# Three attentions of a two-block network on one core: the masks are added on VectorE, in the operation that finds each row's maximum, and no longer by products on TensorE

## What is computed

```
FOX (16 heads of 64): s = q.k * scale + log_f_cum[query] - log_f_cum[key];  keys after the query masked (causal)
MLA (8 heads, query and key of 96, values of 64): s = q.k;   keys of later chunks of 64 masked
SPA (8 heads of 64):  s = q.k;   only the 128 keys with the highest index score of each query are kept
p = softmax(where(mask, s, -inf));   o = p @ v
```

## Time and profile before

| | |
|---|---|
| median of 3 runs | 1862.43 us (1858.46 to 1863.55) |
| profiled execution, its own time | 1852.84 us |
| its span, first to last instruction | 1851.0 us |
| TensorE busy | 1765.5 us, 95% |
| VectorE, ScalarE, GpSimd busy | 666.1, 643.6, 696.8 us |
| mean granted clock of TensorE | 0.987 |

### The profile page before, as it was taken

The page is one execution under the profiler, slowest core; times in us unless marked ns, Lnnn a source line. Parts: engine busy times, 40 slices in busy tenths (PEclk is TensorE's granted clock), DMA queues, the critical chain, the costliest instruction groups (busy, mean ns, idle before and its releaser), DMA issues. The chain is left out here.

```text
span 1851.0 us, 24083 instructions
## 1 busy us (share of the span) xinstructions
PE 1765.5 (95%) x9646; PEld 1488.6 (80%) x9646; DVE 666.1 (36%) x1087; ACT 643.6 (35%) x957; POOL 696.8 (38%) x522
## 2 busy tenths in 40 slices
PE   5999999899999999999999999999999989899999
PEld 5777899688888887878898888888887877668777
DVE  3449236320100013232454400100115179798441
ACT  4643534332222224324333522222225222346440
POOL 2523233254444554543200444444553455620002
PEclk9999999999999999999999999999999999999999
DMA  4112112122322232231200222233222222210001
GB/s 182 69 46 92 69 47 92 57 92 91 108 96 102 91 106 87 103 114 66 74 1 1 92 91 91 92 112 113 91 92 101 92 101 81 93 44 24 1 1 46
DMA packets 22467, 145.40 MB, mean 79 GB/s; under 512 B 2640, under 2 KB 3280, under 8 KB 6384
## 3 DMA queue, kind: packets, MB, share of 16 engines
q1 hardware_dynamic: 22384, 144.22, 21.8%
HBM read 142.05 MB, written 2.10 MB: 78 GB/s over the span
## 5 line engine op out<-in xcount | busy, mean ns | idle before, releaser
L2302 POOL TENSOR_TENSOR wlo<-wraw,whi 128x512 fp32r<-128x512 f32 (+2 forms) x500 | 678.5, 1389 | 1102.1 <-ACT whi L132 1102.1
L132 ACT ACTIVATE whi<-wraw 128x2048 fp32r<-128x2048 f32 (+2 forms) x125 | 235.3, 1883 | 330.5 <-PE PS L329 193.0
L425 PE MATMUL PS<-hT_hi,whi 128*128 128x512 f32 x704 | 274.0, 389 | 0.0
L426 PE MATMUL PS<-hT_lo,whi 128*128 128x512 f32 x704 | 273.9, 389 | 0.0
L427 PE MATMUL PS<-hT_hi,wlo 128*128 128x512 f32 x704 | 273.9, 389 | 0.0
L1511 DVE TENSOR_TENSOR act_sb<-sil,PS 128x512 f32 x44 | 30.3, 688 | 427.4 <-ACT sil L1487 427.4
L425 PEld LDWEIGHTS PS<-hT_hi,whi 128*128 128x128 f32 x704 | 132.2, 188 | 27.5
L427 PEld LDWEIGHTS PS<-hT_hi,wlo 128*128 128x128 f32 x704 | 132.2, 188 | 27.4
L426 PEld LDWEIGHTS PS<-hT_lo,whi 128*128 128x128 f32 x704 | 132.2, 188 | 27.1
L1487 ACT ACTIVATE sil<-PS 128x512 f32<-128x512 f32 x44 | 26.4, 599 | 355.4 <-PE PS L427 335.5
L458 PE MATMUL PS<-whi,hT_hi 128*128 128x512 f32 (+2 forms) x320 | 122.8, 384 | 12.2 <-POOL wlo L2302 4.3
(11 more groups left out here) (366 smaller groups left out, 3164.3 us busy)
## 6 DMA issues: line engine op xcount, KB each, us to landing
wraw<-wpack SPq DMA_DIRECT2D x125, 1024.0 KB, 4.8
gain<-gains SPq DMA_DIRECT2D x10, 512.0 KB, 6.1
x_sb<-x SPq DMA_DIRECT2D x8, 512.0 KB, 7.3
out<-x_sb SPq DMA_DIRECT2D x4, 512.0 KB, 2.6
csb<-consts SPq DMA_DIRECT2D x1, 768.0 KB, 6.7
vlat<-vecs SPq DMA_DIRECT2D x1, 320.0 KB, 3.4
vh<-vecs SPq DMA_DIRECT2D x1, 96.0 KB, 3.9
small<-vecs SPq DMA_DIRECT2D x1, 80.0 KB, 11.5
```

The source lines that it names most:

```text
L132: act.activation(whi[q % 2][:, w], wraw[q % 2][:, w], ACT.Copy).then_inc(w_hi, 1)
L425: nc.tensor.matmul(o, whi[q][w], hT_hi[:, k, :], start=(k == 0), stop=False)
L426: nc.tensor.matmul(o, whi[q][w], hT_lo[:, k, :], start=False, stop=False)
L2302: p.tensor_tensor(wlo[q][:, a:b], wraw[q][:, a:b], whi[q][:, a:b].bitcast(F32), ALU.subtract).then_inc(w_lo, 1)
```

## The change

The mask products are gone, and a unit's scores are one product over all its columns. VectorE's TENSOR_REDUCE becomes a tensor_tensor_reduce: it adds scores and mask, multiplies by -1 and writes the result back in place in PSUM, and writes the minimum over the row (which is the negated maximum) as a second output. exp then reads its input with a scale of -1. For the masks to cover all columns of a unit, FOX and the chunk mask get a tile of 512 columns each, zeros in 384 and the diagonal block in the last 128, of which a unit reads the last (i+1) x 128; VectorE makes them with a memset and a copy each. SPA's mask tiles become float32, the fp32r identities are gone, and the wait for SPA's masks moves from TensorE's to VectorE's queue.

```diff
@@ pe_scores
-                if self.ready and h % 8 == 0 and i:
-                    self.ready(i)
-                full, m = self.mask(i)
                 b, q = self.ring(u)[0], self.q(h, i)
-                n, d = (i + 1) * P, i * P
-                if full:
-                    t.matmul(PS[:, b, 0:n].rearrange("p (j c) -> p j c", c=P), q, self.k(h, 0, i + 1), start=True, stop=False)
-                    t.matmul(PS[:, b, 0:n], identr[:, :], m, start=False, stop=True).then_inc(sem("at_score"), 1)
-                else:
-                    if i:
-                        t.matmul(PS[:, b, 0:d].rearrange("p (j c) -> p j c", c=P), q, self.k(h, 0, i), start=True, stop=True)
-                    t.matmul(PS[:, b, d:n], q, self.k(h, i, i + 1), start=True, stop=False)
-                    t.matmul(PS[:, b, d:n], ident, m, start=False, stop=True).then_inc(sem("at_score"), 1)
+                t.matmul(PS[:, b, 0:(i + 1) * P].rearrange("p (j c) -> p j c", c=P), q, self.k(h, 0, i + 1), start=True,
+                         stop=True).then_inc(sem("at_score"), 1)
@@ exp
-                a.activation(self.pbuf[m][:, 0:n], PS[:, b, 0:n], ACT.Exp, bias=self.nm[:, u % 4:u % 4 + 1],
+                a.activation(self.pbuf[m][:, 0:n], PS[:, b, 0:n], ACT.Exp, bias=self.nm[:, u % 4:u % 4 + 1], scale=-1.0,
                              accum_out=self.rs[:, u:u + 1]).then_inc(sem("at_exp"), 1)
@@ dve_max
-                v.tensor_reduce(self.nm[:, u % 4:u % 4 + 1], PS[:, self.ring(u)[0], 0:(self.units[u][1] + 1) * P], AX_X,
-                                ALU.max, negate=True).then_inc(sem("at_max"), 1)
+                _, i, h = self.units[u]
+                if self.ready and h % 8 == 0 and i:
+                    self.ready(i)
+                s = PS[:, self.ring(u)[0], 0:(i + 1) * P]
+                v.tensor_tensor_reduce(out=s, in0=s, in1=self.mask(i), scale=-1.0, scalar=-MAX_NEG, op0=ALU.add, op1=ALU.min,
+                                       accum_out=self.nm[:, u % 4:u % 4 + 1]).then_inc(sem("at_max"), 1)
@@ setup of the attentions
-        identr = at("identr", AT_JUNK, [P, P], F32R)
+        masks = [at("causal", AT_ARENA + 86 * KB, [P, SEQ]), at("chunks", AT_JUNK + 2 * KB, [P, SEQ])]
+
+        def dve_mask(n, diagonal):
+
+            v = nc.vector
+            v.memset(masks[n][:, 0:SEQ - P], 0.0).then_inc(dve_step, 1)
+            v.tensor_copy(masks[n][:, SEQ - P:SEQ], const(diagonal)).then_inc(dve_step, 1)
+            stepped(2)
+
+        def mask_row(n, i):
+            return masks[n][:, (TT - 1 - i) * P:SEQ]
@@ dve_foxproj
             v.memset(QA[64:66, :, :], 1.0).then_inc(sem("rows1"), 1)
+            dve_mask(0, "negcausal")
             NQ.dve_xn(0)
@@ second block
-        topm = [at(f"topm{i}", AT_XN + 2 * KB * i, [P, SEQ], F32R) for i in range(3)]
+        topm = [at(f"topm{i}", AT_XN + 2 * KB * i, [P, SEQ]) for i in range(3)]
@@ dve_index
-            v.tensor_copy(identr[:, :], ident).then_inc(sem("mask"), 1)
+            dve_mask(1, "negchunk")
@@ mask_a, MLA, SPA (FOX and MLA: lambda i: mask_row(0, i) and mask_row(1, i))
-            return (True, topm[i - 1][:, 0:(i + 1) * P]) if i else (False, const("negchunk"))
+            return topm[i - 1][:, 0:(i + 1) * P] if i else mask_row(1, 0)
-                        ready=lambda i: nc.tensor.wait_ge(sem("mask"), 5 - i))
+                        ready=lambda i: nc.vector.wait_ge(sem("mask"), 4 - i))
```

More of the change, by code:

```diff
@@ L1691, in program @@
                         lambda h, a, b: KA[0:66, h, a * P:b * P].rearrange("p (j c) -> p j c", c=P), lambda h, j: FV[:, j, h * FD:(h + 1) * FD],
-                        lambda i: (False, const("negcausal")),
+                        lambda i: mask_row(0, i),
                         lambda i, b: QA[:, 4 * b:4 * b + 4, i * P:(i + 1) * P].rearrange("p a (b c) -> p a b c", b=2),
@@ L2173, in program @@
         MLA = Attention([FOX], BH, lambda h, i: qb[0:BQ, i, h, :], lambda h, a, b: kb[0:BQ, a:b, h, :],
-                        lambda h, j: vb[:, j, h, :], lambda i: (False, const("negchunk")), out_view, pbuf, ptbuf,
+                        lambda h, j: vb[:, j, h, :], lambda i: mask_row(1, i), out_view, pbuf, ptbuf,
                         after=after_out(1), copies="scalar")
```

## The result

The changed kernel takes **1885.70 us**, the median of 4 runs (1881.17 to 1889.51), beside 1860.45 for the kernel before on the same chip: a ratio of 1.0133, 95% interval 1.0104 to 1.0162. It is slower, by 25 us, where 1846 and a gain were forecast. The profiled execution took 1889.51 us, its span is 1887.7.

What follows compares the result with a forecast made beforehand. TensorE, busy 95% of the span, was taken as the bound, limited in MLA and SPA by the chain ending in ScalarE's copy. Gains 10.2 + 0.6 + 5.9 = 16.7 us off median 1862.43 gave 1846; range 1838 to 1857.

Steps and rivals of the forecast that it cites:

- the one sentence on the clock: Small units: more TensorE waiting might drop the clock to 1.2 GHz, costing a few us, within the range.
- the sum: Gains of FOX, MLA and SPA added: 10.2 + 0.6 + 5.9 = 16.7 us off the median 1862.43.
- TensorE's share in FOX, 0.22 a unit: FOX: dropping two mask passes over 128 columns saves 0.22 us a unit; units of i=3 go from 2.42 to 2.20.
- FOX's units of i=0: FOX's smallest units: no shorter than now; 13 x (0.04 - 0.12) = -1.0 us, 3 x 0.22 = 0.7.
- slack: Time from the end of the copy of turned weights to values(n-2)'s first weight load, less 0.05; zero where TensorE waits.
- x: VectorE's maximum: extra time of the new operation over TENSOR_REDUCE on the chain; 0.12 us, from 0 to 0.25.
- Rival 4: VectorE's new operation runs at half the column rate, adding 0.26 to 0.66 us a unit: 1870 us; chance 0.07.
- rival 3: VectorE's accumulator read-out is dear, 0.25 to 0.4 us: 1853.5 at 0.25, middle 1857; chance 0.15.
- the slower side: Whole kernel: a measured time slower than before, given 0.07; its mechanism was the half column rate on VectorE.
- 5.9 us in the sum: SPA's forecast gain: 2.2, 3.0, 1.0 and -0.3 us for i of 3, 2, 1 and 0.
- 0.6 us in the sum: MLA's forecast gain: 1.1 us for i=3, 0.7 for i=2, -0.6 each for i=1 and i=0.
- 10.2: FOX's forecast gain in us: 10.6 for units of i=3, 2 and 1, with -1.0 and 0.7 for i=0.

Runs made afterwards that it cites:

- MLA by products: Changed kernel with MLA put back to its mask products and plain reduce, FOX and SPA new: 1839.81 us, 0.9893.
- all rows: Changed kernel with score products of all three attentions over 128 rows, query rows beyond the head's own zero: 1829.22 us, 0.9832.
- pause ahead of FOX: Kernel with all score products over 128 rows, TensorE made to wait for six GpSimd fills at the start of FOX: 1843.79 us, 0.9927.
- MLA alone over 128 rows: Changed kernel with only MLA's score products over 128 rows instead of 96, SPA with its 64: 1876.37 us, 1.0093, one execution 1964.31.
- product and sum: Changed kernel with MLA's mask products back on TensorE and VectorE's new operation kept, mask added twice: 1850.94 us, 0.9952.
- FOX over 128 rows: Changed kernel with FOX's score products over 128 rows, MLA as before, SPA new over 64 rows: 1841.01 us, 0.9893.
- second series: Kernel with all score products over 128 rows run once more, 5 runs: 1834.33 us, 0.985 against the kernel before.

## Why the prediction was wrong

**The step that failed** is the one sentence on the clock: "TensorE will wait more in the small units than it does now; should the clock fall to the 1.2 GHz level there, that costs a few us and belongs to the range." It rightly saw that the clock could fall and priced the fall as if the clock came back with the next stretch of work, as it does in the short spells of the projections. The runs show that here the way back is missing: 119.5 us at half rate, from 1718.2 to 1837.7, SPA 94.4 us long for 59.6. The projections' spells are 3.4 and 6.8 us in the kernel before; this one ended when SPA did. I took the clock as a matter of how busy TensorE is, and looked at one stretch at 1.00; what rows the products use did not enter. The sentence of the sum that "nothing in the change touches that difference", the 9.6 us between profiled execution and median, has the same gap: the kernel before took 1853.19 us in an execution at a mean clock of 0.986 and 1863.0 at 0.979, so that difference goes with the clock too.

The Trainium skill, "TensorE: Matmul & The Clock Gate", section on the clock gate (Part 1), says that the lower clock is the default and that sustained activity releases it; by that SPA, 100% busy, should have been at 1.00 soon. This case's rows differ: 25 and 30 us windows busy throughout at 0.50. The same section warns that on this chip the gate has been seen stuck for over 50 us, at a lower level than the half seen here, and tells the reader not to trust the clock's records fully; here the doubled product durations (2.07 us for 1.12) bear the records out.

**The rest, point by point.**
- *TensorE's share in FOX, 0.22 a unit:* right. FOX's units of i=3 went from 2.42 to 2.19 us, of i=2 from 1.88 to 1.65, of i=1 from 1.34 to 1.10.
- *FOX's units of i=0, "no shorter than now":* wrong, to the good. They went from 0.78 to 0.56 and 0.75 in turns, 0.65 on average, which is 2 us over 16 units where a loss of 0.3 stood in the sum. The timeline of the changed kernel, two units of i=0, shows the chain:

```profile
978.30 0.44 PE L1568 MATMUL PS<-KA,QA 66*128 66x128 f32 x2
...
978.78 0.30 DVE L1638 CUSTOM_DVE_ANT_0 PS<-PS,causal 128x128 f32<-128x128 f32 x1 [0.40 <-PE PS L1568]
...
979.00 0.29 DVE L1614 COPY fpt<-PS 128x128 f32<-128x128 f32 x1
...
979.34 0.43 PE L1590 MATMUL PS<-FV,fpt 128*128 128x64 f32 x2
...
979.61 0.44 PE L1568 MATMUL PS<-KA,QA 66*128 66x128 f32 x2
```

  From scores(n) at 978.30 over the sum and the copy to values(n-2) at 979.34 and the scores behind it at 979.61 it is 1.31 us, and in that time two units go by. The chain from scores to maximum held a mask product itself: 0.70 us before (986.07 to 986.77), 0.48 now. I had let each unit gain at most its slack less x; but a chain that is itself shortened by 0.22 and goes round once in two units gives each (0.22 - x)/2. And x is hardly there for the copy, which starts 0.22 after the operation's start (0.21 before), at the same time as the read-out.
- *x = 0.12:* a little high. The operation costs 0.01 more, exp starts 0.07 later. Rival 4, the half rate, and rival 3 are refuted, and with them the only mechanism that I had given the slower side. The result was slower for another reason than the one given.
- *SPA:* 5.9 us in the sum, 5.7 measured where the clock held (MLA by products: 53.9 us for 59.6). That the total agrees is partly luck. By size the forecast was 2.2, 3.0, 1.0 and -0.3 us for i of 3, 2, 1 and 0, and the units gave 2.0, 1.7, 1.2 and 0.8: too much for i=2 and too little for i=0 cancel. A unit of i=3 in its steady turn went from 2.76 to 2.48 us, so 0.28 and not 0.43. I had let the turn start 0.16 us before the end of the score product's record, as in FOX. After a product over 64 rows it starts only 0.07 before, and its record is 0.66 instead of 0.60 (below).
- *MLA:* 0.6 us in the sum, too little. Over 128 rows it took 54.8 us for 55.6 with two short falls in it, and 52.2 with none (all rows, pause ahead of FOX), so 3.4 us at the full clock, of which units with i of 1 and 0, counted at a loss, gave 1.4. The flaw is that of FOX's i=0: the chain held the mask product itself. In the changed kernel MLA cannot be read, the clock being low.
- *The sum:* with FOX and SPA new, MLA as before, the gain is 1859.64 - 1839.81 = 19.8 us, against 10.2 + 5.9 = 16.1 forecast for those two. FOX gave 12.7 for 10.2, nearly all of it in i=0. The unit-by-unit working was right for FOX's units that TensorE limits and too low for those that a chain limits. Had the clock held, the gain would be 12.7 + 3.4 + 5.7, some 22 us, and the time about 1839; this is an estimate from these stages, MLA's part being measured over 128 rows, and it is near the fast end of the range. The working counted instructions at the full rate and left out that the rate itself hung on the kernel's shape.

**What is settled and what is open.** Shown: the long loss needs no new VectorE operation; it is set off behind waits in MLA and inherited by SPA. Under score products over 64 rows a lost clock did not come back within SPA, with or without mask products. Over 66 rows it did not come back within FOX without them, and with them only among FOX's last, smallest units, after 174 us. Over 128 rows it came back within 17 us each time but one, the fall at the very end of MLA in the run with MLA alone over 128 rows, which SPA over 64 rows inherited. Shown too: with its mask products MLA went through waits of 1.3 us and more without a long loss (none in the kernel before and in MLA by products, 3.4 us each in product and sum and with FOX over 128 rows), and its small units' products brought the clock back once. A rival is that rows matter only through the weight loads, which start late behind 64 rows (last section). It doesn't hold for FOX: behind 66 rows they start in the middle of the product (changed kernel: 948.03 in one from 947.65 to 948.51), and the clock did not come back there either. Open: which quantity the chip counts, and why FOX is caught at its first wait only now and then. MLA over 96 rows stands between the two: in its larger units the clock was back after 3.4 to 17 us, in its smaller ones it was not back in the 15 us that the changed kernel has from the fall to SPA. No run varied the rows in steps, and none padded the kernel before alone, mask products kept.

## What to carry to other kernels

Taking small products off TensorE can cost more than they did: the mask products filled MLA's thin stretches, and without them a wait of 1.5 us turned into 119 us at half rate. After such a change read the granted clock by window and compare the duration of one unchanged product, before reading any wait; here a TensorE that was 100% busy was busy because it was slow. Where contractions are over 64 to 96 rows and zero rows are cheap to make, try padding them to 128: here it cost TensorE no time, was worth 56 us against the change alone (1885.70 to 1829.22) and made of it a gain of 1.7% (1.5% in the second series, 1834.33 us).

## What the hardware showed beyond that

**A transpose behind a 64-row product does not get its weights early.** SPA's unit of i=3 over 64 rows (MLA by products) and over 128 rows (all rows), score product and the turn's first weight load:

```profile
1739.07 1.12 PE L1570 MATMUL PS<-ka,qa 64*128 64x512 f32 x2
...
1740.12 0.42 PEld L1593 LDWEIGHTS PS<-csb,pbuf 128*128 128x128 f32 x4 [0.76 <-ACT pbuf L1615]
```

```profile
1737.22 1.08 PE L1572 MATMUL PS<-ka,qo 128*128 128x512 f32 x2
...
1737.70 0.14 PEld L1595 LDWEIGHTS PS<-csb,pbuf 128*128 128x128 f32 x1 [0.24 <-ACT pbuf L1617]
```

Over 64 rows the load starts 0.07 us before the product ends, and so did that of the mask product in the kernel before (1743.63 against 1743.70); over 128 rows it starts in the middle of it, as it does over 66 and 96 rows. A unit takes 2.19 us instead of 2.48, and SPA 49.0 us instead of 53.9. The clock is at 1.00 in both, so 4.9 us of what the padding brings go with the earlier weight loads and not with the clock. Why the loads are late behind 64 rows alone stays open.

**The accumulator of a VectorE operation is cheap here.** Sum, negation, write-back in PSUM and minimum run at the rate of the plain reduce (700 and 692 ns for 512 columns), and the read-out, 142 ns as a record, begins 0.08 us before the operation's record ends, so that the reader starts 0.07 us later than behind the reduce.
